# Hybrid attention and pooling block on one core: transposes of the softmax weights two k-steps later, scores directly ahead of the attention sums, gate parts one step further ahead, a shorter warm-up

## Chip, core and metric

One core of a Trainium2 chip runs the whole kernel. The metric is the device time of one execution in microseconds (us), measured before the change as the median of 3 runs.

## What is computed

The input is x, 2048 rows of 1024 floats. Sixteen learned meta rows stand ahead of them. The reference, cut to what matters:

```python
z = rms_norm(h, norm_gain)                       # 2064 x 1024
q, k, v, g_attn, u_pool, g_pool = split(z @ w_in) # 1024, 128, 128, 1024, 1024, 1024 columns
q, k = partial_rotary(q), partial_rotary(k)      # first 16 of 64 dims of a head
# chunks of 64 rows; keys: the 16 meta rows, the previous chunk, the own chunk
s = q . k / 8;  m = max(max(s), sink)
p = exp(s - m) / (sum(exp(s - m)) + exp(sink - m))
o_attn = p @ v                                   # 16 query heads, 2 key/value heads
o_pool = ((trailing mean over 2/4/8/16 rows of u) - u) @ w_pool * pool_scale
h = h + concat(silu(g_attn) * o_attn, silu(g_pool) * o_pool) @ w_out
out = rms_norm(h, final_gain)[16:]
```

All of it is float32. The kernel keeps that precision with single-pass matmuls by splitting each operand into a high part and the rest (w = wh + wl, z = zh + zl) and adding three products: high by high, high by low, low by high.

## The kernel before

The rows are worked in two halves of 1024 (the loop over `h`). In each half TensorE follows one order that is written out in the code, and the other engines follow theirs; semaphores join them.

*Start.* TensorE runs `WARM` matmuls on zeros (L1172), in a loop of four, and then waits for `ident_in`. `product(g)` (L1189 to L1191) multiplies the pooling map into its projection, once per kernel. It waits for `cu_lo` and `cp_lo`, low parts that VectorE makes (L832 among others) from weights that come by transfer. The normed rows are transposed by `z_transpose` (L1165).

*Stage A* projects keys, values, queries and the gate of the attention. `project(slot, tb, k0, k1)` issues three matmuls of 512 columns for each of the k-steps k0 to k1 (L1123, L1124, L1125), into PSUM bank 6 or 7. `split_hi` on ScalarE (L511) and `split_lo` on VectorE (L782) make the two parts of each block of weights.

*Stage B*, the attention, has 16 steps a half, one for each chunk n of 64 rows, in four groups of four (`sub` 0 to 3). A step does two things at once. It projects one tile of the pooling path (48 matmuls, two blocks `tb` of 8 k-steps), and it takes chunk n through the attention: `transposes` turn the probabilities (L1317, and L1325 for those of the meta rows), `scores` computes the scores of the next chunk (L1282), which use 64 rows of the array each, and the attention sums (L1339, which use 64 columns each, and L1340 for the meta rows) end it. `SOFTMAX_STEPS` is the number of k-steps of the second block that stand ahead of the transposes.

Behind TensorE, the order of ScalarE in a step is: copy the projected block 0, the values (`vw`), the transposed probabilities (`pt`, L721) and the meta ones (`ptm`, L723 and L726), the projected block 1 (L696 or L659), the exponents of the next chunk (L674), one weight split. The order of VectorE is: where `sub` is 1 or 2 the running window sum and the pooling (L965, L971); the denominators and the scaling of the probabilities in two halves (L983 to L991, the second one of L991 sets `p_ready` for the transposes); a gate tile where `sub` is 2 or 3; `split_lo`; the low part of the meta probabilities (L1004, sets `pt_lo`); the maxima of the next chunk's scores (`maxima`, L946 to L951); the second gate tile (L884); the gating of the sums (L1012, sets `o_gate`); where `sub` is 2 or 3, the gating of a pooling tile (L1018). ScalarE adds to `pt_hi` four times per step, two of them for `pt`.

*Stage C*, the output product, is seven products of 8 steps (56 steps, `C_STEPS`). It computes two row groups by two column halves in seven products instead of eight, by sums and differences of gates and weights (`FACTORS`). A step needs 12 matmuls of 512 columns: four row tiles by three part products (L1366, L1367, L1368). For each step `gated_hi(s)` on ScalarE (L742) and `gated_lo(s)` on VectorE (L1029) make the two parts of the gate, in four buffers. ScalarE's `gated_hi(s)` waits until TensorE is through with step s - 4. `step(s)` on TensorE waits for `gs_lo`. Step 0 has its own low part, made by GpSimd (`gsl_first`); step 1 is made when all gating is done. One weight block serves two steps. In the loop over s each of both engines does the split of the block of steps s + 2 and s + 3 (s even), then the gate parts of step s + 2, then smaller work: VectorE adds finished tiles to the residual rows (`add_rows`, L1038), norms the first rows of the next half in product 5 (`z_head`, L798), and scales finished rows in product 6 (`final_rows`, L811 and L818), for which ScalarE takes the statistics (`final_stats`). In the second half the last four steps run by row tiles (`last_steps`), so that tile 0 ends early.

Of the kernel before, what the change touches and what calls it, by code (L numbers as in the profile page):

```python
# [15 lines left out]
KT = D // P  # L16
# [16 lines left out]
EPS = 1e-6  # L33
SOFTMAX_STEPS = 3
WARM = 36
SCALE = HD ** -0.5
# [8 lines left out]
C_STEPS = PRODUCTS * KT  # L45
# [10 lines left out]
def build(nc, x, meta, wa, wu, wb, wp, wq, gain_n, gain_f, consts, ident_d, rot, rot_meta, out):  # L56
# [3 lines left out]
    with ctx:  # L60
# [439 lines left out]
        def _(act):  # L500
# [66 lines left out]
            for h in range(HALVES):  # L567
# [180 lines left out]
                act.wait_ge(p_gate, PT * (h + 1))  # L748
                gated_hi(1)
                for s in range(C_STEPS):  # L750
                    b = s // 2 + 1
                    if s % 2 == 0 and b < C_BLOCKS:
                        split_hi(h, (b,), b % 2)
                    elif s % 2 == 0 and h + 1 < HALVES:
                        split_hi(h + 1, 0, 0)
                    if s + 2 < C_STEPS:
                        gated_hi(s + 2)
                    p, k = divmod(s, KT)
# [9 lines left out]
                    if p == 5 and k < 4 and h + 1 < HALVES:  # L768
                        z_head(h + 1, k)
                    if p == 6 and 3 <= k < 3 + TPG:  # L770
                        final_stats(h, k - 3)
            for t in range(TPG, NTT):
# [4 lines left out]
        def _(dve):  # L777
# [75 lines left out]
            for h in range(HALVES):  # L853
# [172 lines left out]
                def gated_lo(s):  # L1026
                    p, k = divmod(s, KT)
                    dve.wait_ge(gs_hi, C_STEPS * h + s + 1)
                    ve.tensor_tensor(gsl[:, s % 4, :], FACTORS[p][0][:, k, :], gsh[:, s % 4, :].bitcast(F32), ALU.subtract).then_inc(gs_lo, 1)  # L1029
# [9 lines left out]

                gated_lo(1)  # L1040
                for s in range(C_STEPS):
                    b = s // 2 + 1
                    if s % 2 == 0 and (b < C_BLOCKS or h + 1 < HALVES):
                        split_lo(block_c(h, b), b % 2)
                    if s + 2 < C_STEPS:
                        gated_lo(s + 2)
                    p, k = divmod(s, KT)
# [16 lines left out]
                    if p == 3:  # L1064
# [3 lines left out]
                        ve.tensor_tensor(gate_half[1][:, k, :], gate_half[1][:, k, :], gate_half[0][:, k, :], ALU.subtract).then_inc(sum4, 1)  # L1068
                    if p > 0 and k in (1, 3):
                        if p in (1, 3) and k == 1:  # L1070
                            dve.wait_ge(res_in[1 if p == 1 else 0], 16 * TPG * (h + 1))
                        for t in range(k - 1, k + 1):
                            add_rows(p - 1, t)
                    if p == 5 and k < 4 and h + 1 < HALVES:
                        if k == 0:
                            dve.wait_ge(gn_in, 16 * (h + 1))
                        z_head(h + 1, k)
                    if p == 6 and k == 4:
                        dve.wait_ge(f_early, TPG * (h + 1))
                        dve.wait_ge(r_copy, TPG * (h + 1))  # L1080
                        ve.tensor_tensor(f_b1, f_s1, epst.to_broadcast([P, TPG]), ALU.add).then_inc(f_bias, 1)
                    if p == 6 and k >= 4:
                        if k == 4:
                            dve.wait_ge(gf_in, 32 * h + 16)
                        final_rows(h, k - 4)
                for t in range(TPG):
# [7 lines left out]
        def _(pe):  # L1094
# [99 lines left out]
            for h in range(HALVES):  # L1194
# [95 lines left out]
                def attend_group(g, last_group):  # L1290
                    for sub in range(4):
# [34 lines left out]
                        if h == 0 and sub < 2:  # L1326
                            pe.wait_ge(m_ev, 2 + 2 * g + sub + 1)
                        transposes(0).then_inc(t_done, 1)

                        if not (last_group and sub == 3):  # L1330
                            scores(n + 1, 4 * g + sub + 1)
                        project(slot, 1, SOFTMAX_STEPS, KT)

                        pe.wait_ge(pt_lo, n + 1)
                        pe.wait_ge(vw_in, n + 1)
                        ob = ps[:, OB, :]

                        for kv in range(2):
                            te.matmul(ps[kv * HD:kv * HD + HD, OB, :], vw[:, kv, :], pt[:, kv, :], start=True, stop=False)  # L1339
                        te.matmul(ob, vmeta[0:96, :], ptm[0:96, :], start=False, stop=True).then_inc(o_done, 1)  # L1340

# [120 lines left out]
```

## Time and profile before

| | |
|---|---|
| median of 3 runs | 1258.5 us (1258.11 to 1259.89) |
| the profiled execution | 1257.71 us |
| its span | 1255.9 us |
| TensorE busy | 1238.1 us, 99% |
| VectorE, ScalarE, GpSimd busy | 62%, 45%, 14% |
| granted TensorE clock, mean | 0.998 of full speed |

A profile's times come from one execution and count from its first instruction. Matmuls are pipelined, so one of 512 columns shows some 0.39 us busy while the next starts 0.23 us after it: the starts tell the pace. Where a row of the timeline stands for several instructions, its start is that of the first one. A number in brackets at a row's end is how long the engine had been idle, and what ended that.

### The profile page before, as it was taken

What the parts mean: (1) busy time and instruction counts of PE and PEld (TensorE: products, weight loads), DVE (VectorE), ACT (ScalarE), POOL (GpSimd) and SP (SyncE); (2) the same over time, 40 slices, a digit from 0 to 9 for tenths busy, and PEclk for the clock granted to TensorE, in tenths of its full rate; (3) what the DMA queues carried; (4) which work ended last, traced back from release to release, by engine and by line L of the source; (5) the groups of instructions that cost most, each with busy time, mean ns of one, the idle gap of its engine ahead of it and who ended that gap; (6) DMA issues with size and microseconds to landing.
All of it is one profiled execution on the core that took longest, in us unless ns stands there. A gap on an engine that the chain in (4) does not pass through costs nothing.

```text
span 1255.9 us, 16855 instructions
## 1 busy us (share of the span) xinstructions
PE 1238.1 (99%) x6085; PEld 999.0 (80%) x6085; DVE 778.9 (62%) x1240; ACT 570.2 (45%) x1362; POOL 177.9 (14%) x178
## 2 busy tenths in 40 slices
PE   9999999999999999999999999999999999999996
PEld 9788888877777777888788888887777777788885
DVE  6653645567575756957686534436667676695757
ACT  6622222255555555344665222224555555534445
POOL 1154655500000002000011212110000000200000
PEclk9999999999999999999999999999999999999999
DMA  9524444411010112823352211111111111252333
GB/s 356 202 84 160 141 151 134 144 41 35 34 34 34 34 34 80 330 93 118 101 200 74 80 63 36 50 50 34 36 49 34 34 34 34 89 205 92 118 101 151
DMA packets 34153, 122.60 MB, mean 98 GB/s; under 512 B 3568, under 2 KB 3600, under 8 KB 34096
## 3 DMA queue, kind: packets, MB, share of 16 engines
q1 hardware_dynamic: 21408, 74.98, 17.6%
q0 software_dynamic: 12688, 46.83, 10.4%
q8 instruction: 39, 0.64, 0.2%
q14 instruction: 18, 0.15, 0.0%
HBM read 100.83 MB, written 20.97 MB: 97 GB/s over the span
## 4 chain that ended last, share of the span: by engine, by line
PE 94%; DVE 3%; ACT 1%; issue 1%; DMA 1%; DVEq 0%; POOL 0%; ACTq 0%; POOLq 0%
PE ps L1123 20%; PE ps L1124 19%; PE ps L1125 19%; PE ps L1366 7%; PE ps L1367 7%; PE ps L1368 7%; PE ps L1282 3%; PE ps L1339 3%; PE ps L1317 2%; PE ps L1340 1%; PE ps L1165 1%; PE ps L1134 1%; PE ps L1189 1%; PE ps L1190 1%; PE ps L1172 1%; PE ps L1191 1%
## 5 line engine op out<-in xcount | busy, mean ns | idle before, releaser
L1123 PE MATMUL ps<-zh,wsplit 128*128 128x512 f32 x1072 | 422.2, 394 | 0.0
L1124 PE MATMUL ps<-zl,wsplit 128*128 128x512 f32 x1072 | 418.0, 390 | 0.0
L1125 PE MATMUL ps<-zh,wsplit 128*128 128x512 f32 x1072 | 417.8, 390 | 0.0
L782 DVE TENSOR_TENSOR wsplit<-wraw,wsplit 128x1024 fp32r<-128x1024 f32 x124 | 186.7, 1505 | 117.0 <-ACT wsplit L511 116.9
L1123 PEld LDWEIGHTS ps<-zh,wsplit 128*128 128x128 f32 x1072 | 201.3, 188 | 44.7 <-DVE wsplit L782 0.3
L1125 PEld LDWEIGHTS ps<-zh,wsplit 128*128 128x128 f32 x1072 | 201.3, 188 | 42.5
L1124 PEld LDWEIGHTS ps<-zl,wsplit 128*128 128x128 f32 x1072 | 201.3, 188 | 40.8
L511 ACT ACTIVATE wsplit<-wraw 128x1024 fp32r<-128x1024 f32 x124 | 132.4, 1068 | 153.0 <-PE ps L1368 126.6
L1366 PE MATMUL ps<-wsplit,gsh 128*128 128x512 f32 x448 | 174.8, 390 | 3.8 <-DVE gsl L1029 3.7
L1367 PE MATMUL ps<-wsplit,gsh 128*128 128x512 f32 x448 | 174.3, 389 | 0.0
L1368 PE MATMUL ps<-wsplit,gsl 128*128 128x512 f32 x440 | 171.2, 389 | 0.0
L659 ACT ACTIVATE wsum<-ps 128x512 f32<-128x512 f32 x64 | 38.3, 599 | 203.6 <-PE ps L1125 203.6
L1004 DVE TENSOR_TENSOR ptm<-ps,ptm 32x128 fp32r<-32x128 f32 x128 | 36.6, 286 | 114.5 <-ACT ptm L726 113.2
L1366 PEld LDWEIGHTS ps<-wsplit,gsh 128*128 128x128 f32 x448 | 84.1, 188 | 23.5 <-issue 4.4
L1367 PEld LDWEIGHTS ps<-wsplit,gsh 128*128 128x128 f32 x448 | 84.1, 188 | 17.3
L674 ACT ACTIVATE probs<-ps,stat 128x144 f32<-128x144 f32 x256 | 93.8, 390 | 8.7 <-DVE stat L949 8.7
L1368 PEld LDWEIGHTS ps<-wsplit,gsl 128*128 128x128 f32 x440 | 82.6, 188 | 17.1
L406 POOL TENSOR_TENSOR rotsrc<-rotsrc,cos_t 128x1024 f32<-128x1024 f32 x18 | 60.5, 3359 | 223.4 <-DVE swapped L864 223.4
L884 DVE SCALAR_TENSOR_TENSOR gates_all<-wsum,ps 128x512 f32 (+1 forms) x64 | 43.7, 683 | 59.7 <-ACT wsum L659 59.0
L721 ACT ACTIVATE pt<-ps 128x512 f32<-128x512 f32 x64 | 34.8, 595 | 75.2 <-PE ps L1317 75.2
L432 POOL COPY kw<-qk 128x64 f32 (+1 forms) x32 | 8.6, 269 | 412.6 <-PE ps L1282 412.6
L603 ACT ACTIVATE rotsrc<-ps 128x512 f32<-128x512 f32 x32 | 19.1, 598 | 105.2 <-PE ps L1125 105.2
(160 smaller groups left out, 1420.2 us busy)
## 6 DMA issues: line engine op xcount, KB each, us to landing
wraw<-in_wa SPq DMA_DIRECT2D x36, 512.0 KB, 3.5
wraw<-wt SPq DMA_DIRECT2D x32, 512.0 KB, 3.2
wraw<-in_wq SPq DMA_DIRECT2D x24, 512.0 KB, 3.5
tq<-in_wq POOLq DMA_DIRECT2D x8, 1024.0 KB, 6.1
wt<-tq POOLq DMA_DIRECT2D x8, 1024.0 KB, 5.1
wraw<-wc SPq DMA_DIRECT2D x16, 512.0 KB, 3.3
wraw<-in_wb SPq DMA_DIRECT2D x16, 512.0 KB, 3.3
rows<-in_x POOLq DMA_DIRECT2D x16, 512.0 KB, 10.7
```

The lines of the kernel that those rows point to most:

```text
L406: gp.tensor_tensor(rotsrc[:, :], rotsrc[:, :], cos_t[:, :], ALU.mult).then_inc(rot_cos, 1)
L511: sc.activation(wh[:, slot, 0:size], wraw[:, slot, 0:size], ACT.Copy).then_inc(w_hi, 1)
L659: sc.activation(wsum[:, tb * TB:tb * TB + TB], ps[:, PB[tb], :], ACT.Tanh, scale=0.5).then_inc(tanh_r, 1)
L674: i = sc.activation(probs[:, u, kv * KEYS:kv * KEYS + KEYS], score_tile(u, kv), ACT.Exp, bias=negm[:, 4 * kv + u:4 * kv + u + 1], scale=SCALE,
L782: ve.tensor_tensor(wl[:, slot, 0:size], wraw[:, slot, 0:size], wh[:, slot, 0:size].bitcast(F32), ALU.subtract).then_inc(w_lo, 1)
L884: ve.scalar_tensor_tensor(dst, wsum[:, tb * TB:tb * TB + TB], 1.0, ps[:, PB[tb], :], ALU.add, ALU.mult).then_inc(pb_free[tb], 1)
L1123: te.matmul(ps[:, PB[bank], :], w_h, rhs_z(zh, tb, k), start=k == 0, stop=False)
L1124: te.matmul(ps[:, PB[bank], :], w_h, rhs_z(zl, tb, k), start=False, stop=False)
L1125: last = te.matmul(ps[:, PB[bank], :], w_l, rhs_z(zh, tb, k), start=False, stop=k == KT - 1)
L1366: te.matmul(c_bank(p, t), g_h, w_h, start=ANEW[p] and k == 0, stop=False, skip_group_check=True)
L1367: te.matmul(c_bank(p, t), g_h, w_l, start=False, stop=False, skip_group_check=True)
L1368: last = te.matmul(c_bank(p, t), g_l, w_h, start=False, stop=k == KT - 1, skip_group_check=True)
```

## The change

Four things are changed.

1. `SOFTMAX_STEPS` goes from 3 to 5: five k-steps of the second block stand ahead of the transposes and three behind. `scores(n + 1)` moves from directly behind the transposes to behind those three, directly ahead of the attention sums. The first two matmuls of the sums wait for the copies `pt` alone (`pt_hi`), and the wait for `pt_lo` moves to the last one.
2. `gated_hi` and `gated_lo` are made for step s + 3 in iteration s, no more for s + 2.
3. In stage C `add_rows` moves to steps 0 and 1 of a product (from 1 and 3), and the statistics and the scaling of finished rows in product 6 come two steps sooner.
4. `WARM` goes from 36 to 28.

```diff
--- before.py
+++ after.py
@@ -31,8 +31,8 @@
 KPITCH = KEYS + META
 META0 = 2 * CH
 EPS = 1e-6
-SOFTMAX_STEPS = 3
-WARM = 36
+SOFTMAX_STEPS = 5
+WARM = 28
 SCALE = HD ** -0.5
 PRE = 32
 
@@ -747,14 +747,15 @@
                 act.wait_ge(pb_free[1], FREES * (h + 1) + CREDIT)
                 act.wait_ge(p_gate, PT * (h + 1))
                 gated_hi(1)
+                gated_hi(2)
                 for s in range(C_STEPS):
                     b = s // 2 + 1
                     if s % 2 == 0 and b < C_BLOCKS:
                         split_hi(h, (b,), b % 2)
                     elif s % 2 == 0 and h + 1 < HALVES:
                         split_hi(h + 1, 0, 0)
-                    if s + 2 < C_STEPS:
-                        gated_hi(s + 2)
+                    if s + 3 < C_STEPS:
+                        gated_hi(s + 3)
                     p, k = divmod(s, KT)
                     if p == 4 and k % 2 == 1:
 
@@ -767,8 +768,8 @@
                         act.wait_ge(f_early, TPG * h + t + 1)
                     if p == 5 and k < 4 and h + 1 < HALVES:
                         z_head(h + 1, k)
-                    if p == 6 and 3 <= k < 3 + TPG:
-                        final_stats(h, k - 3)
+                    if p == 6 and 1 <= k < 1 + TPG:
+                        final_stats(h, k - 1)
             for t in range(TPG, NTT):
                 final_stats(HALVES - 1, t)
 
@@ -1038,12 +1039,13 @@
                         ve.tensor_tensor(rows[1][t][:, 1, :] if p == 6 else there, c_bank(p, t), there, ALU.add).then_inc(h_add, 1)
 
                 gated_lo(1)
+                gated_lo(2)
                 for s in range(C_STEPS):
                     b = s // 2 + 1
                     if s % 2 == 0 and (b < C_BLOCKS or h + 1 < HALVES):
                         split_lo(block_c(h, b), b % 2)
-                    if s + 2 < C_STEPS:
-                        gated_lo(s + 2)
+                    if s + 3 < C_STEPS:
+                        gated_lo(s + 3)
                     p, k = divmod(s, KT)
                     if p == 0:
                         if k == 0:
@@ -1066,23 +1068,23 @@
                         if k == 0:
                             dve.wait_ge(sum2, KT * (h + 1))
                         ve.tensor_tensor(gate_half[1][:, k, :], gate_half[1][:, k, :], gate_half[0][:, k, :], ALU.subtract).then_inc(sum4, 1)
-                    if p > 0 and k in (1, 3):
-                        if p in (1, 3) and k == 1:
+                    if p > 0 and k in (0, 1):
+                        if p in (1, 3) and k == 0:
                             dve.wait_ge(res_in[1 if p == 1 else 0], 16 * TPG * (h + 1))
-                        for t in range(k - 1, k + 1):
+                        for t in range(2 * k, 2 * k + 2):
                             add_rows(p - 1, t)
                     if p == 5 and k < 4 and h + 1 < HALVES:
                         if k == 0:
                             dve.wait_ge(gn_in, 16 * (h + 1))
                         z_head(h + 1, k)
-                    if p == 6 and k == 4:
+                    if p == 6 and k == 2:
                         dve.wait_ge(f_early, TPG * (h + 1))
                         dve.wait_ge(r_copy, TPG * (h + 1))
                         ve.tensor_tensor(f_b1, f_s1, epst.to_broadcast([P, TPG]), ALU.add).then_inc(f_bias, 1)
-                    if p == 6 and k >= 4:
-                        if k == 4:
+                    if p == 6 and 2 <= k < 2 + TPG:
+                        if k == 2:
                             dve.wait_ge(gf_in, 32 * h + 16)
-                        final_rows(h, k - 4)
+                        final_rows(h, k - 2)
                 for t in range(TPG):
                     add_rows(PRODUCTS - 1, t)
                     if h + 1 == HALVES and t > 0:
@@ -1326,17 +1328,18 @@
                         if h == 0 and sub < 2:
                             pe.wait_ge(m_ev, 2 + 2 * g + sub + 1)
                         transposes(0).then_inc(t_done, 1)
+                        project(slot, 1, SOFTMAX_STEPS, KT)
+
 
                         if not (last_group and sub == 3):
                             scores(n + 1, 4 * g + sub + 1)
-                        project(slot, 1, SOFTMAX_STEPS, KT)
-
-                        pe.wait_ge(pt_lo, n + 1)
+                        pe.wait_ge(pt_hi, 4 * n + 2)
                         pe.wait_ge(vw_in, n + 1)
                         ob = ps[:, OB, :]
 
                         for kv in range(2):
                             te.matmul(ps[kv * HD:kv * HD + HD, OB, :], vw[:, kv, :], pt[:, kv, :], start=True, stop=False)
+                        pe.wait_ge(pt_lo, n + 1)
                         te.matmul(ob, vmeta[0:96, :], ptm[0:96, :], start=False, stop=True).then_inc(o_done, 1)
 
                 for g in range(NG):
```

Two places in the order of the instructions. The first is TensorE in the attention, chunk 16 (the first of the second half), from the last matmul of the fifth or third k-step of the second block. `probs` are the probabilities, `pmeta` those of the meta rows, `kw` the keys of the window. Before:

```order
L1125 MATMUL ps<-zh,wsplit 128x512
L1317 MATMUL ps<-ident,probs 128x128 [waits o_gate,p_ready]
L1317 MATMUL ps<-ident,probs 128x128 x3
L1325 MATMUL ps<-ident,pmeta 128x128 [waits u_in]
L1317 MATMUL ps<-ident,probs 128x128 x4
L1282 MATMUL ps<-kw,qk 128x144 [waits ks_in]
L1282 MATMUL ps<-kw,qk 128x144 x7
L1123 MATMUL ps<-zh,wsplit 128x512
...
L1125 MATMUL ps<-zh,wsplit 128x512
L1339 MATMUL ps<-pt,vw 64x512 [waits vw_in,pt_lo]
L1339 MATMUL ps<-pt,vw 64x512
L1340 MATMUL ps<-ptm,vmeta 128x512
```

And in the changed kernel, whose lines are numbered two or three higher:

```order
L1127 MATMUL ps<-zh,wsplit 128x512
L1319 MATMUL ps<-ident,probs 128x128 [waits o_gate,p_ready]
L1319 MATMUL ps<-ident,probs 128x128 x3
L1327 MATMUL ps<-ident,pmeta 128x128 [waits u_in]
L1319 MATMUL ps<-ident,probs 128x128 x4
L1125 MATMUL ps<-zh,wsplit 128x512
...
L1127 MATMUL ps<-zh,wsplit 128x512
L1284 MATMUL ps<-kw,qk 128x144 [waits ks_in]
L1284 MATMUL ps<-kw,qk 128x144 x7
L1341 MATMUL ps<-pt,vw 64x512 [waits vw_in,pt_hi]
L1341 MATMUL ps<-pt,vw 64x512
L1343 MATMUL ps<-ptm,vmeta 128x512 [waits pt_lo]
```

The scores have left the place between transposes and projections (15 matmuls stood behind them there, 9 stand now behind the transposes) for the one ahead of the sums.

The second is VectorE at the end of the second half, from the steps of product 6 to the first addition of the last product. `gsl` are low parts of gates, `wsplit` the last weight block. Before:

```order
L782 TENSOR_TENSOR wsplit<-wraw,wsplit 128x1024 [waits w_hi]
L1029 TENSOR_TENSOR gsl<-gates_all,gsh 128x512 [waits gs_hi]
L1081 TENSOR_TENSOR stat<-stat,small 128x4 [waits r_copy,f_early]
L811 RECIPROCAL stat<-stat 128x1 [waits f_std,gf_in]
L818 SCALAR_TENSOR_TENSOR rows_51<-rows_51,stat,gainf 128x1024 [waits f_rstd]
L1029 TENSOR_TENSOR gsl<-gates_all,gsh 128x512 [waits gs_hi]
L811 RECIPROCAL stat<-stat 128x1 [waits f_std]
L818 SCALAR_TENSOR_TENSOR rows_51<-rows_51,stat,gainf 128x1024 [waits f_rstd]
```

And in the changed kernel:

```order
L1083 TENSOR_TENSOR stat<-stat,small 128x4 [waits r_copy,f_early]
L812 RECIPROCAL stat<-stat 128x1 [waits f_std,gf_in]
L819 SCALAR_TENSOR_TENSOR rows_51<-rows_51,stat,gainf 128x1024 [waits f_rstd]
L1030 TENSOR_TENSOR gsl<-gates_all,gsh 128x512 [waits gs_hi]
L812 RECIPROCAL stat<-stat 128x1 [waits f_std]
L819 SCALAR_TENSOR_TENSOR rows_51<-rows_51,stat,gainf 128x1024 [waits f_rstd]
L783 TENSOR_TENSOR wsplit<-wraw,wsplit 128x1024 [waits w_hi]
L1030 TENSOR_TENSOR gsl<-gates_all,gsh 128x512 [waits gs_hi]
```

Two scaled rows and the gate part of step 54 now stand ahead of the last weight split, and the gate part of step 55 directly behind it.

## Rows read from the trace of the kernel before

**Rows 1.** the page, busy time of each engine and its share.

```profile
PE 1238.1 (99%) x6085; PEld 999.0 (80%) x6085; DVE 778.9 (62%) x1240; ACT 570.2 (45%) x1362; POOL 177.9 (14%) x178
```

**Rows 2.** waits of TensorE: instruction, releaser, us in total, times, longest.

```profile
PE ps L1366 <- DVE gsl L1029: 3.7, 5, 1.1
PE ps L1165 <- DVE xr L798: 1.5, 2, 1.3
PE ps L1339 <- DVE ptm L1004: 1.2, 2, 0.6
...
PE ps L1165 <- DVE gates_all L1038: 0.5, 1, 0.5
```

**Rows 3.** timeline of TensorE, chunk 16: start, us busy, line, out<-in, shape.

```profile
864.90 0.60 PE L1317 MATMUL ps<-ident,probs 128*128 128x128 f32 x4
865.43 1.25 PE L1282 MATMUL ps<-kw,qk 64*128 64x144 f32 x16
866.61 0.50 PE L1123 MATMUL ps<-zh,wsplit 128*128 128x512 f32 x1
866.95 0.39 PE L1124 MATMUL ps<-zl,wsplit 128*128 128x512 f32 x1
...
869.92 0.39 PE L1125 MATMUL ps<-zh,wsplit 128*128 128x512 f32 x1
870.24 1.08 PE L1339 MATMUL ps<-pt,vw 128*64 128x512 f32 x4
871.25 0.50 PE L1340 MATMUL ps<-ptm,vmeta 96*128 96x512 f32 x1
```

**Rows 4.** timeline of TensorE, the last chunk.

```profile
1086.00 0.60 PE L1317 MATMUL ps<-ident,probs 128*128 128x128 f32 x4
1086.36 0.48 PE L1123 MATMUL ps<-zh,wsplit 128*128 128x512 f32 x1
1086.67 0.40 PE L1124 MATMUL ps<-zl,wsplit 128*128 128x512 f32 x1
```

**Rows 5.** timeline of VectorE, chunk 16.

```profile
868.30 1.19 DVE L1004 TENSOR_TENSOR ptm<-ps,ptm 32x128 fp32r<-32x128 f32 x4 [4.25 <-ACT ptm L726]
...
871.11 0.17 DVE L951 TENSOR_TENSOR stat<-stat,cst 128x8 f32<-128x8 f32 x1
871.89 0.69 DVE L1012 SCALAR_TENSOR_TENSOR gates_all<-ps,gates_all 128x512 f32 x1 [0.62 <-PE ps L1340]
```

**Rows 6.** timelines of VectorE and TensorE, chunk 17.

```profile
877.96 0.68 DVE L991 TENSOR_TENSOR probs<-probs,stat 128x512 f32<-128x512 f32 x1
...
879.10 0.60 PE L1317 MATMUL ps<-ident,probs 128*128 128x128 f32 x4
```

**Rows 7.** timeline of TensorE, product 5 of the first half.

```profile
622.82 0.47 PE L1366 MATMUL ps<-wsplit,gsh 128*128 128x512 f32 x1 [0.60 <-DVE gsl L1029]
```

**Rows 8.** timelines of VectorE and, last, TensorE at the end.

```profile
1235.83 1.23 DVE L782 TENSOR_TENSOR wsplit<-wraw,wsplit 128x1024 fp32r<-128x1024 f32 x1 [1.81 <-ACT wsplit L511]
...
1242.62 1.29 DVE L818 SCALAR_TENSOR_TENSOR rows<-rows,stat,gainf 128x1024 f32<-128x1024 f32 x1
...
1251.20 1.42 DVE L818 SCALAR_TENSOR_TENSOR gates_all<-gates_all,stat 128x512 f32<-128x512 f32 x2
...
1239.87 0.47 PE L1366 MATMUL ps<-wsplit,gsh 128*128 128x512 f32 x1 [1.14 <-DVE gsl L1029]
```

**Rows 9.** timelines of VectorE and TensorE at the start.

```profile
6.76 1.23 DVE L832 TENSOR_TENSOR cul<-curaw,cuh 128x1024 fp32r<-128x1024 f32 x1 [2.21 <-ACT cuh L555]
...
1.10 7.94 PE L1172 MATMUL ps<-warm 128*128 128x160 f32 x36 [1.10 <-POOL warm L359]
...
8.84 0.49 PE L1189 MATMUL ps<-cph,cuh 128*128 128x256 f32 x1
...
12.09 0.28 PE L1189 MATMUL ps<-cph,cuh 128*128 128x256 f32 x1
...
12.21 0.28 PE L1190 MATMUL ps<-cpl,cuh 128*128 128x256 f32 x1
```

## The prediction, made before the result was known

> **What bounds the kernel now.** I read the page first. TensorE is busy for 1238.1 us of the span of 1255.9 us, 99% [rows 1]; VectorE, the next, for 62%. So no other engine is the bound on average, and a gain must come from TensorE's few pauses or from the spacing of its own matmuls. The profiled execution took 1257.71 us, 1.8 us more than its span and 0.8 us under the median of the three runs, 1258.5 us.
>
> The waits of TensorE come next [rows 2]. The output product (L1366) waits five times for the low part of a gate, 3.7 us in all; the attention sums (L1339) wait twice, 0.6 us each, for the low part of the transposed meta probabilities.
>
> A busy share hides spacing, so I read TensorE's timeline of one attention step [rows 3]. Projections of 512 columns start 0.228 us apart (13 steps from 866.95 to 869.92). Around the small matmuls it is more. From the last four transposes to the scores: 0.53. From the scores to the first projection behind them: 1.18. From that one to the next: 0.34, which is 0.11 over the usual. From the last projection to the sums: 0.32, 0.09 over. The last chunk of a half has no scores left to compute, and there a projection follows the transposes directly: 0.36, and then 0.31 to the next [rows 4]. So each change of kind has a price, and the change alters which kinds are neighbours.
>
> **The attention step (30 of 32).** Per step nothing is added or removed on TensorE: 48 projections, 9 transposes, the scores, the sums. Neighbours before: transposes to scores, scores to projection and its follower, projection to sums: 0.53 + 1.18 + 0.34 + 0.32 = 2.37 [rows 3]. After: transposes to projection and its follower, 0.36 + 0.31 [rows 4]; projection to scores, for which I take the 0.32 of projection to sums, since both go from the full array to a tiled one; and scores to sums, which no row shows. The nearest row is scores to projection, 1.18. The weights of the sums are exposed already where they follow a projection, so I add nothing for them. The upper bound is 1.18 + 0.13, a surcharge like the two in this step, 0.09 and 0.11, rounded up; the lower is 1.17. The sum is 2.17, so 0.20 less per step (0.07 at the upper bound): **30 x 0.20 = 6.0 us**, between 2.1 and 6.3.
>
> What queues behind the moved work: the transposes stand two k-steps of three matmuls, 1.37 us, later. From the start of the last four the chain over ScalarE's copies to the end of VectorE's L1004 takes 4.59 us (869.49 less 864.90) [rows 3, 5]. The last matmul of the sums (L1340), the only one that still waits for it, now stands 0.36 + 0.31 + 1.60 + 0.32 + 1.18 + 1.01 = 4.78 us behind the same start. It fits by 0.13 us, if the semaphore takes 0.06: thin.
>
> VectorE's maxima stand behind L1004 in its queue, so they begin 1.37 us later, and scores that come later cost nothing as long as L1004 opens them. The gating of the sums (L1012) waits for TensorE now and starts at 871.89; in the new order the queue reaches it 1.79 us behind L1004's end (871.28 less 869.49), that is 0.76 later against the same base [rows 5]. The scaled probabilities of the next chunk are ready at 878.64 and their transposes start at 879.10, 0.46 us of slack, about the least of all steps [rows 6]. Transposes come 1.37 - 0.20 later and the queue 0.76, so the slack grows to 0.9 us.
>
> **The last chunk of each half (2 times).** Its sums have no scores ahead. They waited for the low part and then took 1.01 us to L1340; now L1340 alone waits. The low part comes 1.37 us later, so L1340 starts 1.37 - 1.01 = 0.36 us later. The gating, the second gating (L1018), the split of gate 1 and the second product step follow in a chain, all on VectorE and ScalarE: with what queues before it, 0.4 each, **+0.8 us**. This chain, and not the depth of the lead, is why two of the five waits of L1366 (0.8 each) stay.
>
> **Gate parts one product step further ahead.** The work is the same. In product 5 of the first half VectorE carries the next rows' norm (four passes of 1.28 us) beside four additions, two weight splits and four gate parts, in four steps of 12 x 0.228 = 2.73 us. It falls behind: a wait of 0.60 us at 622.82 [rows 7], 0.25 of spacing before it, and 0.08 of exposed weight load behind each. One more step of lead is 2.73 us, more than the 1.0 us that are missing: **-1.1 us** (0.6 to 1.2). The nearest deadline then is the split for steps 44 and 45, met by some 0.2 us.
>
> At the end of the second half the last four steps are ordered by tiles and need gates 54 and 55 early. The two waits there are the rest of rows 2, 3.7 - 1.6 - 0.6 = 1.5 us, the longer one 1.14 [rows 2, 8]. Gate 54 now comes before the last weight split and gate 55 directly behind it, with no final row between. With 0.16 of exposed loads and what the waits hide of the spacing that is 2.0 us, less 0.2, as a final row now delays that split a little. The kernel's end, though, is VectorE's: from that split at 1235.83 to the last row at 1252.62 its queue has one pause of 0.5 us. Two final rows (1.28 us and a reciprocal, 1.4 each) and one gate part (0.6) move ahead of the split, into a stretch of which 1.81 us were idle [rows 8]. 2.8 + 0.6 - 0.3 = 3.1, and TensorE, 1.8 us sooner, is just in time for the last addition: **-3.1 us** (1.4 to 3.3).
>
> Between the halves four additions start late behind two final rows, and TensorE waits 0.5 us [rows 2]. That wait goes, but the next norms hang on transfers: **-0.3 us** (0 to 0.6). The residual rows are needed one step earlier than now and are there.
>
> **Warm-up, 36 to 28 matmuls.** Eight of them at 7.94 / 36 = 0.22 us are 1.7 us [rows 9]. But the first product needs a VectorE pass that ends at 7.99, so TensorE idles for some 0.9 us and starts 0.8 us sooner than 8.84 [rows 9]. Later it waits up to 1.3 us for rows that come by transfer (L1165 [rows 2]), which takes the gain back. I count **0**, between -0.7 and +1.5.
>
> **Sum.** -6.0 + 0.8 - 1.1 - 3.1 - 0.3 + 0 = -9.7 us: 1257.7 becomes 1248.0; from the median, 1248.8. I say **1248.3**.
>
> **Rivals.**
> *The sums pay a surcharge of their own* (0.18). The scores use half the rows of the array and the sums half its columns, so the change between them may cost what the others do: 0.13 x 30 = 3.9 us, giving 1252.2. Against it: the 1.18 to a projection already holds such a change. The Trainium skill ("TensorEngine Tiling (Array Packing)", Key Properties) says that changing the tiling mode drains TensorE. By that rule this neighbourhood pays too; the trace agrees that every change shown costs extra [rows 3], and no row shows this one.
> *The low part comes late* (0.10). If L1340 waits in each step for more than the 0.13 us of margin, the gain of the step shrinks by as much; at 0.2 us of wait the attention gains nothing: 1254.3.
> *The lead does not help* (0.08). The waits of the gates shift instead of going, and of the 4.5 us of those terms 3.5 are lost: 1251.8.
> *The clock rises later* (0.07). The first products start 0.217 us apart, (12.09 - 8.84)/15, and then 0.12 [rows 9], the granted clock at its lower level and at its upper. Were the 33 matmuls that follow in the first product at the lower level too, 3 us would be lost: 1251.3. The idle 0.9 us speaks for it; that the rise came 3.2 us behind the first product, and not in 8 us of warm-up, against. The Trainium skill ("TensorE: Matmul & The Clock Gate", Part 1) says that the throttled rate is the default and that activity releases it. The trace agrees; by that rule fewer warm-up matmuls can only delay the release.
> *Slower: VectorE's queue becomes the bound* (0.04). Maxima, gating, window sum and probabilities stand in one queue. In the 16 steps with a window sum ahead, each us that it ends behind the transposes' turn costs 16 us: 0.65 us take all the gain, 0.8 us give 1261. It needs the queue 1.7 us later than I work out.
> The forecast has the rest, 0.53.
>
> **How the numbers follow.** A measurement here tells about 0.2%, 2.5 us, from no change. Forecast and first four rivals are faster by more, save 0.03 for the second and third together: faster 0.93, same 0.03, slower 0.04. The range takes in the forecast with its bounds and the rivals at 1252.2, 1251.8 and 1251.3, so 1245.5 to 1253.0; the late low part and the slower case, 0.14, are left out.
>
> **What would show it.** Scores to sums 1.2 us apart, and steps of 14.54 us where they were 14.74 in the second half, from one chunk's first transposes to the next's; no wait before L1340 save in the last chunks, about 1 us; the waits of L1366 down to the two of 0.8; a last row some 3 us sooner; a pause behind the warm-up. I am wrong if steps take 14.7 us or more, if transposes wait for probabilities, or if VectorE's end is as far behind the last matmul as now.

## The result, and the profile after

The changed kernel takes 1247.69 us, the median of 4 runs (1246.68 to 1249.33), against 1258.66 us before (4 runs, 1258.11 to 1259.89). The ratio is 0.9914, with a 95% interval of 0.9899 to 0.9928: 11 us, or 0.9%, less. The forecast was 1248.3 us, in a range of 1245.5 to 1253.0.

The profiled execution took 1246.68 us. Its page gives the span and the busy times; TensorE is at 99% again, so its busy time fell with the span:

```profile
span 1244.9 us, 16835 instructions
...
PE 1229.7 (99%) x6077; PEld 996.8 (80%) x6077; DVE 779.5 (63%) x1240; ACT 575.0 (46%) x1362; POOL 178.0 (14%) x178
```

Lines are numbered one to three higher than before. The waits of TensorE (instruction, releaser, us in total, times, longest), which answer to [rows 2]:

```profile
PE ps L1343 <- DVE ptm L1005: 1.9, 2, 0.9
PE ps L1369 <- DVE gsl L1030: 1.7, 2, 0.8
...
PE ps L1167 <- DVE xr L799: 0.9, 1, 0.9
PE ps L1167 <- DVE zl L804: 0.7, 1, 0.7
...
PE ps L1191 <- DVE cul L833: 0.4, 1, 0.4
PE ps L1369 <- DVE wsplit L783: 0.2, 1, 0.2
```

The output product (L1369) waits for gate parts twice, not five times: the two of 0.8 us are left. 0.2 us for the last weight split is new. The sums no longer wait at their first matmul but at the one for the meta rows (L1343), in the two last chunks alone, 0.9 us each. Of the transposes of rows (L1167), one now waits 0.7 us for `zl`, where it waited 0.5 us for the additions.

One attention step, chunk 17, on TensorE's timeline (start, us busy, line), answers to [rows 3]:

```profile
875.33 0.60 PE L1319 MATMUL ps<-ident,probs 128*128 128x128 f32 x4
875.69 0.48 PE L1125 MATMUL ps<-zh,wsplit 128*128 128x512 f32 x1
876.00 0.40 PE L1126 MATMUL ps<-zl,wsplit 128*128 128x512 f32 x1
...
877.63 0.40 PE L1127 MATMUL ps<-zh,wsplit 128*128 128x512 f32 x1
877.95 1.25 PE L1284 MATMUL ps<-kw,qk 64*128 64x144 f32 x16
879.13 1.08 PE L1341 MATMUL ps<-pt,vw 128*64 128x512 f32 x4
880.14 0.50 PE L1343 MATMUL ps<-ptm,vmeta 96*128 96x512 f32 x1
```

Transposes to projection 0.36 and 0.31; projection to scores 0.32; scores to sums 1.18, exactly what scores to projection was; sums to the meta matmul 1.01. No wait stands in it. VectorE in the same step and its next probabilities answer to [rows 5, 6]:

```profile
878.73 1.19 DVE L1005 TENSOR_TENSOR ptm<-ps,ptm 32x128 fp32r<-32x128 f32 x4 [3.72 <-ACT ptm L726]
879.94 1.36 DVE L947 TENSOR_REDUCE stat<-ps 128x8 f32<-128x1152 f32 x1
...
881.67 0.69 DVE L1013 SCALAR_TENSOR_TENSOR gates_all<-ps,gates_all 128x512 f32 x1
...
887.54 0.69 DVE L992 TENSOR_TENSOR probs<-probs,stat 128x512 f32<-128x512 f32 x1
```

The low part (L1005) ends at 879.92, 4.59 us behind the last transposes' start, as before, and L1343 starts 0.22 us after it (0.20 in the tightest steps). The maxima follow at once, and the gating (L1013) stands directly behind them without a wait for TensorE. The next probabilities end at 888.23; their transposes start at 889.33. (These are chunk 18's, with 1.1 us of slack; the least of any chunk is 0.91 us, for chunk 17, where it was 0.46.)

The last chunk and the second product step, which answer to [rows 4]:

```profile
1081.47 1.08 PE L1341 MATMUL ps<-pt,vw 128*64 128x512 f32 x4
1083.48 0.50 PE L1343 MATMUL ps<-ptm,vmeta 96*128 96x512 f32 x1 [0.93 <-DVE ptm L1005]
...
1087.55 0.47 PE L1369 MATMUL ps<-wsplit,gsh 128*128 128x512 f32 x1 [0.84 <-DVE gsl L1030]
```

The sums' first two matmuls run early, and the third waits until the low part is there: 2.01 us from L1341 to L1343 instead of 1.01.

The end, VectorE and then TensorE's last matmul, against [rows 8]:

```profile
1228.18 1.22 DVE L783 TENSOR_TENSOR wsplit<-wraw,wsplit 128x1024 fp32r<-128x1024 f32 x1
...
1237.98 0.69 DVE L1039 TENSOR_TENSOR gates_all<-ps,rows 128x512 f32<-128x512 f32 x1
...
1240.17 1.42 DVE L819 SCALAR_TENSOR_TENSOR gates_all<-gates_all,stat 128x512 f32<-128x512 f32 x2
```

```profile
1237.56 0.39 PE L1371 MATMUL ps<-wsplit,gsl 128*128 128x512 f32 x1
```

The last row ends at 1241.59, 4.03 us behind the start of the last matmul. Before, it ended at 1252.62 and the last matmul started at 1247.25: 5.37 us.

The same by stage, in us, from the profiles of before and of the change. Stages run from one first or last instruction to another: the start up to the first scores; each half's attention from there to the first matmul of its output product; each output product to its last matmul (the first one to the transposes behind it); the projections of the second half up to its first scores; the rest up to VectorE's last row.

| stage | before | after | difference | forecast |
|---|---|---|---|---|
| start, to the first scores | 245.42 | 243.72 | -1.70 | 0 |
| attention, first half | 250.07 | 247.17 | -2.90 | -2.6 |
| output product, first half | 154.63 | 153.45 | -1.18 | -1.1 |
| transposes and projections, second half | 205.39 | 205.71 | +0.32 | -0.3 |
| attention, second half | 236.47 | 233.76 | -2.71 | -2.6 |
| output product, second half | 155.25 | 153.75 | -1.50 | -1.8 |
| last matmul to last row | 5.37 | 4.03 | -1.34 | -1.3 |

The stages behind the start give 9.3 us of the 11.0, against 9.7 forecast. The other 1.7 us are the start's, and no run below ties them to the change.

### The profile page after: what moved, and what is told of

Its sections match the earlier page's. It is cut to its first block, busy times and chain, and to the rows that moved or that the text cites. A ratio compares the mean times of both kernels' runs of the same rounds, so it can differ in the third digit from the quotient of the medians.

```text
span 1244.9 us, 16835 instructions
## 1 busy us (share of the span) xinstructions
PE 1229.7 (99%) x6077; PEld 996.8 (80%) x6077; DVE 779.5 (63%) x1240; ACT 575.0 (46%) x1362; POOL 178.0 (14%) x178
## 4 chain that ended last, share of the span: by engine, by line
PE 95%; DVE 2%; ACT 1%; DMA 1%; issue 0%; DVEq 0%; SPq 0%; ACTq 0%
PE ps L1125 20%; PE ps L1126 19%; PE ps L1127 19%; PE ps L1369 7%; PE ps L1371 7%; PE ps L1370 7%; PE ps L1284 3%; PE ps L1341 2%; PE ps L1319 2%; PE ps L1343 1%; PE ps L1167 1%; PE ps L1136 1%; PE ps L1191 1%; PE ps L1192 1%; PE ps L1193 1%; DMA xr<-in_x 1%
## 5 line engine op out<-in xcount | busy, mean ns | idle before, releaser
L1369 PE MATMUL ps<-wsplit,gsh 128*128 128x512 f32 x448 | 174.6, 390 | 1.9 <-DVE gsl L1030 1.7
L1005 DVE TENSOR_TENSOR ptm<-ps,ptm 32x128 fp32r<-32x128 f32 x128 | 36.6, 286 | 131.3 <-ACT ptm L726 129.9
L1369 PEld LDWEIGHTS ps<-wsplit,gsh 128*128 128x128 f32 x448 | 84.1, 188 | 20.4 <-issue 2.5
L742 ACT ACTIVATE gsh<-gates_all 128x512 fp32r<-128x512 f32 x94 | 58.1, 622 | 47.6 <-PE ps L1371 41.1
L1030 DVE TENSOR_TENSOR gsl<-gates_all,gsh 128x512 fp32r<-128x512 f32 x94 | 64.2, 686 | 7.9 <-ACT gsh L742 7.9
```

The lines of the kernel that those rows point to most:

```text
L742: sc.activation(gsh[:, s % 4, :], FACTORS[p][0][:, k, :], ACT.Copy).then_inc(gs_hi, 1)
L1369: te.matmul(c_bank(p, t), g_h, w_h, start=ANEW[p] and k == 0, stop=False, skip_group_check=True)
```

## The experiments

Each run gives a median and, beside it, the stages of its profile. Its ratio is to runs of the kernel before that were taken beside it, whose medians were 1258.5 us for e1, e2, e3 and e7, 1258.96 for e5, e6, e8 and e9, and 1258.76 for e10 and e11. These stages are far steadier than the whole: the attention of the second half was 236.47 or 236.48 us in every kernel that left it alone. Two stages are not steady: the start, from 243.7 to 247.3 us among the five kernels with 28 warm-up matmuls, which are alike there, and the stage between, from 205.3 to 206.1. The stage between goes with a transfer: ScalarE waits in it for rows that arrive, by at most 0.2 us where the stage takes 205.3 to 205.5, and by 1.0 us in e2, e3 and e7, where it takes 206.1.

| kernel | median, us | ratio to before, 95% | start | attention 1, 2 | product 1 | between | product 2 | tail |
|---|---|---|---|---|---|---|---|---|
| before | | | 245.42 | 250.07, 236.47 | 154.63 | 205.39 | 155.25 | 5.37 |
| the change | 1247.69 | 0.9914 (0.9899 to 0.9928) | 243.72 | 247.17, 233.76 | 153.45 | 205.71 | 153.75 | 4.03 |
| e1 | 1257.99 | 0.9997 (0.9988 to 1.0007) | 246.99 | 250.07, 236.47 | 154.68 | 205.46 | 155.26 | 5.36 |
| e2 | 1259.11 | 1.0005 (0.9995 to 1.0015) | 245.97 | 250.26, 236.82 | 154.65 | 206.12 | 155.26 | 5.37 |
| e3 | 1253.16 | 0.9955 (0.9939 to 0.9972) | 246.02 | 247.00, 233.75 | 154.68 | 206.12 | 155.22 | 5.36 |
| e7 | 1254.25 | 0.9960 (0.9947 to 0.9972) | 246.31 | 250.08, 236.48 | 153.43 | 206.09 | 153.74 | 4.03 |
| e5 | 1258.43 | 0.9990 (0.9981 to 1.0000) | 246.85 | 250.08, 236.47 | 154.00 | 206.04 | 153.65 | 6.81 |
| e6 | 1256.49 | 0.9983 (0.9973 to 0.9992) | 246.19 | 250.08, 236.47 | 153.76 | 205.30 | 155.66 | 4.03 |
| e8 | 1245.99 | 0.9899 (0.9883 to 0.9916) | 244.71 | 246.37, 233.02 | 153.41 | 205.37 | 153.73 | 4.03 |
| e9 | 1279.28, one run | | 247.31 | 261.28, 247.75 | 153.78 | 205.87 | 154.15 | 4.03 |
| e10 | 1248.64 | 0.9922 (0.9906 to 0.9939) | 244.17 | 247.18, 233.76 | 153.44 | 205.78 | 153.75 | 4.03 |
| e11 | 1244.66 | 0.9883 (0.9866 to 0.9899) | 246.83 | 246.34, 233.06 | 152.54 | 205.34 | 152.87 | 4.03 |

The theory under test, that of the neighbours: the attention gains because other kinds of matmul now follow each other and these changes cost less, not because a wait goes. Its rival, that of the room: later transposes and a later wait for the low part take waits away that the trace shows badly.

**e2, later transposes without moving the scores.**

```diff
-SOFTMAX_STEPS = 3
+SOFTMAX_STEPS = 5
...
-pe.wait_ge(pt_lo, n + 1)
+pe.wait_ge(pt_hi, 4 * n + 2)
...
+pe.wait_ge(pt_lo, n + 1)
 te.matmul(ob, vmeta[0:96, :], ptm[0:96, :], start=False, stop=True)
```

> The kernel before with five k-steps ahead of the transposes and the wait for the low part at the last matmul of the sums, but with the scores left directly behind the transposes. Theory of the neighbours (the gain of the attention comes from which kinds of matmul follow each other): no neighbour changes, so steps stay at 14.74 us, and the last chunks cost 0.8 us: 1259.3. Theory of the room (it comes from waits that the later transposes take away): the attention gains most of its 6 us here, 1253 or less.

No gain: 1.0005 of before (0.9995 to 1.0015). Steps stayed at 14.74 us, and the two attention stages are 0.19 and 0.35 us longer. The last chunk costs some 0.34 us in each half; in the first half the steps that also carry meta rows give 0.16 us of it back. The room alone is worth nothing; this rival falls.

**e3, the scores moved and nothing else.**

```diff
-if not (last_group and sub == 3):
-    scores(n + 1, 4 * g + sub + 1)
 project(slot, 1, SOFTMAX_STEPS, KT)
+if not (last_group and sub == 3):
+    scores(n + 1, 4 * g + sub + 1)
```

> The kernel before with the scores moved directly ahead of the sums and nothing else: transposes behind three k-steps, low part waited for at the first matmul of the sums. Theory of the neighbours: scores to sums 1.18 us, steps of 14.54 us, 30 x 0.20 = 6.0 us less and nothing lost in the last chunks: 1252.5. By my account of VectorE's queue the slack of the probabilities shrinks to 0.2 us and holds. Theory of the room: without later transposes the probabilities or the low part come late, steps of 14.7 us or more, 1257 to 1262.

1253.16 us, 0.9955 (0.9939 to 0.9972). The attention stages are 3.07 and 2.72 us shorter, 5.8 us together, as much as in the change. TensorE's timeline of chunk 17:

```profile
877.73 0.60 PE L1317 MATMUL ps<-ident,probs 128*128 128x128 f32 x4
...
881.71 1.25 PE L1282 MATMUL ps<-kw,qk 64*128 64x144 f32 x16
882.89 1.08 PE L1339 MATMUL ps<-pt,vw 128*64 128x512 f32 x4
883.90 0.50 PE L1340 MATMUL ps<-ptm,vmeta 96*128 96x512 f32 x1
```

From the last transposes to the sums 5.16 us pass, with scores to sums at 1.18 as in the change. The low part, which needs 4.59 us, was never late even at the first matmul. The other side of it is VectorE's slack, here the second pass over the probabilities and the first transposes of the same chunk:

```profile
876.22 0.68 DVE L991 TENSOR_TENSOR probs<-probs,stat 128x512 f32<-128x512 f32 x1
```

```profile
877.19 0.60 PE L1317 MATMUL ps<-ident,probs 128*128 128x128 f32 x4
```

The probabilities end at 876.90 and the transposes start at 877.19: 0.29 us, which holds. So `SOFTMAX_STEPS = 5` and the split of the wait are not what gains; moving the scores is.

**e9, the low part waited for first, in the changed kernel.** What the split of the wait is for:

```diff
-pe.wait_ge(pt_hi, 4 * n + 2)
+pe.wait_ge(pt_lo, n + 1)
...
-pe.wait_ge(pt_lo, n + 1)
 te.matmul(ob, vmeta[0:96, :], ptm[0:96, :], start=False, stop=True)
```

> The changed kernel, but the first matmul of the sums waits for the low part again. The low part is there 4.32 us behind the last transpose and the first matmul's turn is at 3.47, so each of 30 steps waits 0.85 us and the last chunks 1.0 more than now: 27.5 us slower than the change, steps of 15.39 us, 1275. Rival: if the sums' first matmuls are held by something else already (ScalarE's copies), nothing changes.

One run, 1279.28 us. Start, timeline of TensorE, chunk 18:

```profile
894.38 0.60 PE L1319 MATMUL ps<-ident,probs 128*128 128x128 f32 x4
...
896.98 1.25 PE L1284 MATMUL ps<-kw,qk 64*128 64x144 f32 x16
899.02 1.08 PE L1341 MATMUL ps<-pt,vw 128*64 128x512 f32 x4 [0.79 <-DVE ptm L1005]
```

Scores to sums is 2.04 us instead of 1.18, with a wait of 0.79 for the low part, and steps are 15.39 us as expected. The two attention stages grow by 14.1 and 14.0 us, 28.1 in all (27.5 expected). Most of the rest over 1275 is the start, 3.6 us longer in this profile; the output products are 0.33 and 0.40 us longer too. With transposes two k-steps later, the split wait is a condition, not a gain of its own.

**e8, three k-steps again in the changed kernel.** If the room is not needed, the later transposes only cost:

```diff
-SOFTMAX_STEPS = 5
+SOFTMAX_STEPS = 3
```

> The changed kernel with three k-steps ahead of the transposes again, all else as changed (scores directly ahead of the sums, low part waited for at the last matmul of the sums). Theory of the neighbours: steps stay at 14.54 us as in the change. The last chunks: from the last transpose to L1343 4.63 us, over the 4.32 that the low part takes, so the wait of 0.93 us goes and each ends 1.05 us sooner: 2.1 us less than the change, 1245.6. Rival: the later transposes were needed; the probabilities' slack of 0.2 to 0.3 us does not hold and the steps grow, 1248 or more.

1245.99 us, the median of 4; 0.9899 of before (0.9883 to 0.9916), an interval that overlaps the change's. The profile settles what the medians leave open: the attention stages are 0.80 and 0.74 us shorter than in the change, 1.5 us together where 2.1 were expected. The last chunks give 2.0 of that, and the steps take 0.5 us back, most of them being 14.56 us long and not 14.53 or 14.54; why is not shown. The waits of TensorE:

```profile
PE ps L1369 <- DVE gsl L1030: 1.6, 2, 0.8
PE ps L1167 <- DVE xr L799: 1.5, 2, 1.3
```

No wait for the low part is left in the list, in any chunk, while the two of the second product step stay as they were:

```profile
1086.59 0.47 PE L1369 MATMUL ps<-wsplit,gsh 128*128 128x512 f32 x1 [0.79 <-DVE gsl L1030]
```

**e7, the output product's part of the change alone; e5 and e6, its two halves.** e5 is the lead:

```diff
 gated_hi(1)
+gated_hi(2)
...
-if s + 2 < C_STEPS:
-    gated_hi(s + 2)
+if s + 3 < C_STEPS:
+    gated_hi(s + 3)
```

and the same for `gated_lo`. e6 is the other half, at the lead of before: `add_rows` in steps 0 and 1 of a product, statistics and final rows of product 6 two steps sooner. e7 has both.

> The kernel before with the whole of the change to the output product (gate parts three steps ahead, additions and final rows earlier) and nothing of the attention or the warm-up. My terms: 1.1 for product 5, 3.1 at the end, 0.3 between the halves, 4.5 in all: 1254.0; the waits of the output product down from five to the two of 0.8. By the profile of the change, 1.2 + 2.8 = 4.0 us. If the terms overlap with the attention's, under 2 us.

> The kernel before with the gate parts three steps ahead and nothing else. If the lead is what takes the waits away: product 5 of the first half gains 1.1 us and the two waits at the end (1.85 us of spacing) go, but VectorE's queue behind the last weight split is shorter by one gate part alone, so the last row ends only 0.6 us sooner at the end: 1.7 us in all, 1256.8. If TensorE and not VectorE sets the end, 3 us or more, 1255.4.

> The kernel before with additions and final rows earlier and the gate parts two steps ahead as before. The waits of the output product stay about as they are (3.7 us, the split of rows and gates being as tight), and the last matmul does not move; the end of VectorE's queue comes nearer to it: the last row ends 3.7 us behind the last matmul's end where it ended 5.0 behind: 1.3 us, 1257.2. If VectorE's queue alone sets the end, 2.8 us, 1255.7.

e7 came to 1254.25 us (0.9960, 0.9947 to 0.9972). Its stages are those of the change: 1.20, 1.51 and 1.34 us less. e5 is at the edge of what can be told, 0.9990 (0.9981 to 1.0000), e6 at 0.9983 (0.9973 to 0.9992). The stages tell more. At the end the two are not a sum:

| against before | last product | tail | together |
|---|---|---|---|
| e5, lead | -1.60 | +1.44 | -0.16 |
| e6, rows early | +0.41 | -1.34 | -0.93 |
| e7, both | -1.51 | -1.34 | -2.85 |

With the lead alone TensorE ends 1.6 us sooner, and VectorE ends as late as ever. This is VectorE's end in e5, whose last matmul starts at 1247.09:

```profile
1250.30 0.68 DVE L1039 TENSOR_TENSOR gates_all<-ps,rows 128x512 f32<-128x512 f32 x1
...
1252.48 1.42 DVE L819 SCALAR_TENSOR_TENSOR gates_all<-gates_all,stat 128x512 f32<-128x512 f32 x2
```

Its last addition starts 3.2 us behind the start of the last matmul; in the change it starts 0.42 behind. With the rows alone VectorE is ready sooner, and TensorE is not. Here each engine is the bound as soon as the other is not.

In product 5 of the first half the same: e5 gains 0.63 us there, e6 0.87, both 1.20. In e5 the wait of 0.60 us for the gate is gone and one of 0.29 us for the weight split stands in its place; in e6, at the old lead, no wait is listed there. So the additions had a share in the 1.1 us that I had given to the lead alone. Both expectations missed this: e5 was to gain 1.1 us there and 0.6 at the end and gained 0.63 and 0.16; e6 was to gain nothing there and 1.3 at the end and gained 0.87 and 0.93.

**e11, gate 1 made before the wait for the pooling tiles,** on top of e8. It tries the cause of the two waits that stay:

```diff
-act.wait_ge(p_gate, PT * (h + 1))
 gated_hi(1)
+act.wait_ge(p_gate, PT * (h + 1))
 gated_hi(2)
```

> The changed kernel with three k-steps ahead of the transposes, and with ScalarE's high part of gate 1 made before its wait for the gated pooling tiles (p_gate) and not after it. The two waits of 0.8 us at the second product step hang on a chain: gating of the sums, gating of the pooling tile (L1018, 1.28 us), high part on ScalarE (0.63), low part on VectorE (0.69). If that is the cause, ScalarE's part now runs beside the gating of the pooling tile and each wait falls by 0.6 us to 0.2: 1.2 us under e8_steps3, 1244.7. If the wait is VectorE's alone, nothing changes, 1246.0.

ScalarE, then VectorE, at the second half's second product step:

```profile
1085.04 0.63 ACT L742 ACTIVATE gsh<-gates_all 128x512 fp32r<-128x512 f32 x1 [1.57 <-DVE gates_all L1013]
```

```profile
1084.31 0.69 DVE L1013 SCALAR_TENSOR_TENSOR gates_all<-ps,gates_all 128x512 f32<-128x512 f32 x1
1084.92 1.28 DVE L1019 SCALAR_TENSOR_TENSOR gates_all<-pooled,stat,gates_all 128x1024 f32<-128x1024 f32 x1
1086.11 1.48 DVE L1030 TENSOR_TENSOR gsl<-gates_all,gsh 128x512 fp32r<-128x512 f32 x2
```

The high part (1085.04) now runs beside the gating of the pooling tile (1084.92), and the low part follows that at once. Both waits have left the list; the output products are 0.87 and 0.86 us shorter than in e8. The median is 1244.66 us, 0.9883 (0.9866 to 0.9899): this is the best version found, better than both kernels of the comparison by its interval to before and, against the change, by its stages (3.7 us less from the first scores to the end); the two intervals to before touch at 0.9899.

**e1 and e10, the warm-up.** e1 is the kernel before with `WARM = 28`, e10 the changed one with `WARM = 4`.

> The kernel before with the shorter warm-up alone. My count was 0: TensorE starts the first product some 0.8 us sooner and gives it back at the rows that come by transfer. The profile of the change, though, has the first scores 1.7 us sooner. If that is the warm-up, this run is 1.0 to 1.7 us faster and its first scores start near 243.8 us; if it was chance in the transfers, 0 to 0.5 us, first scores near 245. The rival of the clock that rises later gives 1 to 3 us slower.

> The changed kernel with 4 warm-up matmuls where it has 28. The first product starts when its low part is there, near 7.7 us, with or without them. If the warm-up brings the rise of the granted clock forward, it now comes later than the 10.4 to 16 us seen so far, and every us of delay costs 0.4 us at the first scores: 1 to 3 us slower than the change. If the rise hangs on what comes behind the warm-up, 1247.7 as the change, with the same scatter.

e1: 1257.99 us, 0.9997 (0.9988 to 1.0007), so no effect that can be told, and its first scores start at 246.99, later than before's. e10: 1248.64 us against the change's 1247.69, with intervals that overlap. The 1.7 us that the change's profile has at the start are thus not shown to be the warm-up's, nor anything else's.

## Why the prediction was right, point by point

*The attention step.* Right, down to the price of the neighbourhood that no row showed: 1.18 us from scores to sums. 0.20 us per step were forecast, and the steps went from 14.74 to 14.54. The rival of a surcharge there fell. What the forecast didn't see is that the change's own later transposes are not needed for this (e3), and cost 1.5 us (e8).

*The margin of the low part.* Forecast 0.13 us. L1343 starts 0.20 to 0.23 us behind the end of L1005. In the last chunks, where it waits, it starts 0.05 to 0.06 behind, so the margin is 0.14 to 0.18. Thin, and it held in all 30 steps; the rival of the late low part did not come.

*VectorE's queue.* Forecast: 0.9 us of slack at the transposes; measured: 0.91 in the tightest step. The rival in which this queue becomes the bound did not come either.

*The last chunks.* Forecast +0.8 us for both. From the first chunk's transposes to the last chunk's the steps gave 3.24 and 3.06 us, 6.3 where 6.0 were forecast (the steps that also carry meta rows gave up to 0.23 each), and the stages gave 2.90 and 2.71. That leaves 0.34 us a half, 0.7 for both, and e2 shows the same 0.34. Slightly too high, and made up for by the steps.

*The lead.* "One more step of lead is 2.73 us, more than the 1.0 us that are missing": the size was right (1.1 forecast, 1.18 measured) and the attribution was not: the lead alone gains 0.63 us (e5) and the earlier additions alone 0.87 (e6). That the size came out is in part luck.

*The end.* 3.1 us forecast, 2.84 measured (1.50 on TensorE, 1.34 behind it). The working, two queues that must both become shorter, is what e5 and e6 show.

*Between the halves.* This step failed: -0.3 forecast, +0.32 measured. "That wait goes" was true. The third group of transposes no longer waits for the additions; the fourth waits 0.72 us for a low part instead:

```profile
644.34 2.78 PE L1167 MATMUL ps<-ident,xr 128*128 128x128 f32 x24
647.84 1.07 PE L1167 MATMUL ps<-ident,xr 128*128 128x128 f32 x8 [0.72 <-DVE zl L804]
```

That low part is made from the first group's copy, and its distance did not change: the fourth group starts 3.50 us behind the first, where it started 3.53 behind it before. Behind that the stage hangs on a transfer: ScalarE waits 0.51 us for rows in the change and not at all in e8. e8, the same kernel in this place, has 205.37, which is no difference to before. The gain of 0.3 us was not there, and the 0.32 us are within what this stage scatters.

*The start.* "I count 0" was the forecast, the profile has -1.70, and e1 says that the warm-up explains none of it that can be told. Single profiles differ by more than that. The first product started 1.14 us sooner, behind a pause of 0.36 us, where 0.8 and 0.9 were forecast. The rival of the later clock is not settled: in the change the clock rose at 11.1 us, 0.9 sooner than before, but in three of the five kernels with 28 warm-up matmuls it rose at 16 us or later (last section).

*The total.* The medians differ by 11.0 us and 10.2 were forecast (1258.5 to 1248.3). Without the start the profiles give 9.3 where the terms said 9.7. That the median fell within 0.6 us of the forecast is in part luck: the start gave 1.7 us that no term had. The range is not the sum of the terms' bounds either, though the prediction says that it takes them in: taken together, these reach from 1247.2 to 1256.7, counted from the median.

## What to carry to other kernels

Where TensorE is busy all the time, read the starts of its matmuls at each change of kind and add up what each pair of neighbours costs: here moving one block of small matmuls next to another was worth 5.8 us with nothing taken away. Where two engines finish a kernel together, make both queues shorter at once, for either alone gave 0.2 or 0.9 us of the 2.9. And a wait that is taken away in front of a chain that has its own length only moves: look for what the next instruction needs before counting it.

## What the runs showed of the hardware that was not expected

The time at which TensorE's granted clock rose to its upper level differed between profiles. The number of warm-up matmuls alone does not order it: it rose at 10.3 to 13.6 us in the six kernels with 36, at 11.3 with 4, at 11.1 and 12.2 in two kernels with 28 and at 15.9 to 16.7 in the other three with 28. With 4 warm-up matmuls (e10) TensorE was idle for 5 us and started its products at 7.26; their pace went from 0.21 to 0.12 us some 4 us later:

```profile
1.10 1.11 PE L1174 MATMUL ps<-warm 128*128 128x160 f32 x4 [1.10 <-POOL warm L359]
7.26 0.55 PE L1191 MATMUL ps<-cph,cuh 128*128 128x256 f32 x1 [5.04 <-DVE cul L833]
...
11.24 0.31 PE L1191 MATMUL ps<-cph,cuh 128*128 128x256 f32 x1
11.39 0.28 PE L1192 MATMUL ps<-cpl,cuh 128*128 128x256 f32 x1
```

With 28 (e1) it was idle for 0.77 us in the middle of the first product, waiting for the low part of the second weight, and the pace changed only at 15.9:

```profile
10.03 0.41 PE L1191 MATMUL ps<-cph,cul 128*128 128x256 f32 x1
11.21 0.58 PE L1189 MATMUL ps<-cph,cuh 128*128 128x256 f32 x1 [0.77 <-DVE cul L832]
...
15.86 0.32 PE L1189 MATMUL ps<-cph,cuh 128*128 128x256 f32 x1
16.02 0.28 PE L1190 MATMUL ps<-cpl,cuh 128*128 128x256 f32 x1
```

In the three late ones (e1, e9, e11) TensorE paused for 0.5 to 0.8 us near 10 to 11 us, inside the product; in the other nine it did not pause there. All three have 28 warm-up matmuls; so a shorter warm-up may bring the products to the point where they meet a late low part. That the pause is the cause is only argued; no run tried it by itself. The last matmul of the product started at 36.4 to 36.6 us in those three and at 33.7 to 35.5 in the others; the first scores started at 246.8 to 247.3 and at 243.7 to 246.9, so the rise is not all that moves the start.

In three profiles (e2, e5, e6) the granted clock fell again during the waits for rows near 48 us, while TensorE was issuing. Here e6 (window, its length, busy us, instructions, granted clock as a share of the upper level, DMA share, GB/s):

```profile
40.00:47.80 7.80, 5.34 (x35) 1.00 0.95 366
48.00:51.00 3.00, 3.00 (x8) 0.50 0.58 193
52.00:56.00 4.00, 4.00 (x24) 1.00 0.00 0
```

Ahead of the fall TensorE had been busy for 5.34 of 7.80 us. The other kernels wait there as well, without a fall; e7 was busy for 5.28 of the same 7.80 us. In e9, with its wait in each attention step, the clock also fell at 508 and 1116 us, behind the last chunks' wait of 1.97 us, for 3.4 us each time. Runs of one kernel scatter by some 2 to 4 us. Part of that goes with the clock: in e5 the three runs with a mean granted clock of 0.996 took 1258.8 to 1259.6 us and the six with 0.998 took 1256.7 to 1258.4. How much the start as a whole makes of the scatter is not shown, but it is the stage that varies most between profiles, and so changes of 1 us were read from stages and not from medians.
